# Filler products ahead of five attention stages, done as pairs on two halves of the PE array

## What is computed

```python
s = einsum('bqhgd,bkhd->bhgqk', qb, kb) * scale
p = softmax(where(mask, s, NEG))
o = einsum('bhgqk,bkhd->bqhgd', p, vb)
```

## Time and profile before

| | |
|---|---|
| median of 3 runs | 2260.39 us (2255.84 to 2262.58) |
| profiled execution, span | 2259.5 us |
| TensorE products busy | 2103.5 us, 93% |
| TensorE weight loads busy | 1715.7 us |
| VectorE busy | 894.1 us |
| ScalarE busy | 582.4 us |
| GpSimd busy | 1071.8 us |
| mean granted TensorE clock | 0.943 |

### The profile page before, as it was taken

How to read it: one execution, slowest core, us unless ns; L and a number is a source line. 1 busy time by engine, 2 the same in 40 slices (tenths; PEclk the granted TensorE clock), 3 DMA queues, 4 the chain that set the end, 5 groups by cost and what they waited for, 6 DMA issues and landing times.

```text
span 2259.5 us, 30914 instructions
## 1 busy us (share of the span) xinstructions
PE 2103.5 (93%) x10410; PEld 1715.7 (76%) x10420; DVE 894.1 (40%) x1703; ACT 582.4 (26%) x1432; POOL 1071.8 (47%) x688
## 2 busy tenths in 40 slices
PE   5776999789999989879999999999999999999999
PEld 4665676678888878766678888887787888888887
DVE  4663567264434015546654221201362644221200
ACT  2111556232222003336532011100132642011100
POOL 4443003257666655400135666665553036666664
PEclk9887998889999999988579999999999999999999
DMA  4222001113333322110012333332221013333322
GB/s 132 66 61 66 0 0 38 47 57 111 93 95 119 93 77 82 54 38 1 0 47 84 103 98 97 93 94 84 79 85 62 1 38 94 103 101 94 94 94 91
DMA packets 125209, 161.90 MB, mean 72 GB/s; under 512 B 11511, under 2 KB 87239, under 8 KB 125127
## 3 DMA queue, kind: packets, MB, share of 16 engines
q1 hardware_dynamic: 121440, 159.97, 23.0%
q10 hardware_dynamic: 3686, 0.82, 0.2%
HBM read 158.66 MB, written 2.10 MB: 71 GB/s over the span
## 4 chain that ended last, share of the span: by engine, by line
PE 87%; DVE 7%; ACT 2%; issue 2%; DMA 1%; POOL 1%; ACTq 0%; SPq 0%; DVEq 0%; POOLq 0%
PE ps L588 22%; PE ps L589 22%; PE ps L590 22%; PE ps L875 7%; PE ps L896 5%; PE ps L887 3%; PE ps L603 2%; PE ps L721 2%; PE ps L880 1%; DVE tok L1540 1%; PE ps L903 1%; DVE xt_lo L1550 1%; PE ps L1003 1%; DVE rstd L1516 1%; ACT dump L1114 1%
## 5 line engine op out<-in xcount | busy, mean ns | idle before, releaser
L420 POOL TENSOR_TENSOR w_lo<-raw,w_hi 128x1024 fp32r<-128x1024 f32 (+1 forms) x256 | 616.6, 2409 | 21.3
L418 POOL TENSOR_SCALAR w_hi<-raw 128x1024 fp32r<-128x1024 f32 (+1 forms) x256 | 275.0, 1074 | 557.6 <-PE ps L590 536.7
L588 PE MATMUL ps<-xt_hi,w_hi 128*128 128x512 f32 (+1 forms) x1160 | 433.6, 374 | 7.2 <-DVE xt_lo L1550 6.5
L589 PE MATMUL ps<-xt_lo,w_hi 128*128 128x512 f32 (+1 forms) x1160 | 432.7, 373 | 0.0
L590 PE MATMUL ps<-xt_hi,w_lo 128*128 128x512 f32 (+1 forms) x1160 | 432.6, 373 | 0.0
L588 PE MATMUL ps<-w_hi,xt_hi 128*128 128x512 f32 (+3 forms) x672 | 264.6, 394 | 28.3 <-ACT tok L1374 18.3
L589 PE MATMUL ps<-w_lo,xt_hi 128*128 128x512 f32 (+3 forms) x672 | 260.4, 387 | 0.0
L590 PE MATMUL ps<-w_hi,xt_lo 128*128 128x512 f32 (+3 forms) x672 | 260.1, 387 | 0.0
L588 PEld LDWEIGHTS ps<-xt_hi,w_hi 128*128 128x128 f32 x1160 | 219.8, 189 | 47.4 <-DVE xt_lo L1550 7.6
L590 PEld LDWEIGHTS ps<-xt_hi,w_lo 128*128 128x128 f32 x1160 | 219.6, 189 | 38.5
L589 PEld LDWEIGHTS ps<-xt_lo,w_hi 128*128 128x128 f32 x1160 | 219.7, 189 | 38.2
(11 more groups left out here) (268 smaller groups left out, 2799.1 us busy)
## 6 DMA issues: line engine op xcount, KB each, us to landing
raw<-in_w_up SPq DMA_DIRECT2D x88, 256.0 KB
raw<-in_l_w_gate SPq DMA_DIRECT2D x88, 256.0 KB
raw<-in_l_w_up SPq DMA_DIRECT2D x88, 256.0 KB
raw<-in_l_w_down SPq DMA_DIRECT2D x40, 512.0 KB
raw<-in_l_w_in SPq DMA_DIRECT2D x36, 512.0 KB
raw<-in_w_down SPq DMA_DIRECT2D x20, 512.0 KB
raw<-in_l_w_o SPq DMA_DIRECT2D x16, 512.0 KB
raw<-in_w_in SPq DMA_DIRECT2D x12, 512.0 KB
```

Of the source, the lines that this page charges most:

```text
L418: e.tensor_scalar(w_hi[:, s, 0:width], r, 1.0, 0.0, ALU.mult, ALU.add).then_inc(split, 1)
L420: e.tensor_tensor(w_lo[:, s, 0:width], r, w_hi[:, s, 0:width].bitcast(F32), ALU.subtract).then_inc(split, 1)
L588: e.matmul(o, s_hi, m_hi, start=start, stop=False)
L589: e.matmul(o, s_hi, m_lo, start=False, stop=False)
```

## The change

`fill(FILL, bank(6))` ahead of a stage becomes `warm(cfg["warm"])`, with a kind for each stage. All kinds write to PSUM places that nobody reads before they are overwritten. `low` and `high` are partitions (or columns) 0 to 63 and 64 to 127.

- nsa, "rows": four times two f32 products with 64 rows each, one from the low and one from the high partitions of `h`, 512 columns, into banks 6 and 7.
- swa, "columns": four times two f32 products with 64 stationary columns each, into the low and high partitions of bank 6, 512 columns.
- att2, "rounded": as "rows", from `ckv_hi`, which is fp32r.
- stk, "masked": twice two f32 products as in "rows", then a bf16 product of the identity with the mask onto each bank.
- fox, "steps": as "columns", but with 512, 384, 256 and 128 columns, two products each.

The fillers inside stk stay as they are. Nothing else changes.

```diff
--- before.py
+++ after.py
@@ -902,6 +902,32 @@
             for _ in range(times):
                 e.matmul(place, ident_b[:, :], dump[:, 0:W], start=True, stop=True)
 
+        def warm(kind):
+
+            low, high = slice(0, HD), slice(HD, P)
+            if kind == "rows":
+                for _ in range(FILL // 2):
+                    for b, half in ((6, low), (7, high)):
+                        e.matmul(bank(b), h[half, 0, 0:P], h[half, 0, 0:W], start=True, stop=True)
+            elif kind == "columns":
+                for _ in range(FILL // 2):
+                    for half in (low, high):
+                        e.matmul(ps[half, 6 * W:7 * W], h[:, 0, half], h[:, 1, 0:W], start=True, stop=True)
+            elif kind == "rounded":
+                for _ in range(FILL // 2):
+                    for b, half in ((6, low), (7, high)):
+                        e.matmul(bank(b), ckv_hi[half, 0:P], ckv_hi[half, :], start=True, stop=True)
+            elif kind == "masked":
+                for _ in range(FILL // 4):
+                    for b, half in ((6, low), (7, high)):
+                        e.matmul(bank(b), h[half, 0, 0:P], h[half, 0, 0:W], start=True, stop=False)
+                    for b in (6, 7):
+                        e.matmul(bank(b, P), ident_b[:, :], cfg["mask"][:, :], start=False, stop=True)
+            else:
+                for n in (4, 3, 2, 1):
+                    for half in (low, high):
+                        e.matmul(ps[half, 6 * W:6 * W + n * P], h[:, 0, half], h[:, 1, 0:n * P], start=True, stop=True)
+
         for s, v in cfg.get("start", ()):
             e.wait_ge(s, v)
         e.sem_inc(sem(f"{name}_pv"), 2)
@@ -909,7 +935,7 @@
             scores(0, k)
         for s, v in cfg["banks"]:
             e.wait_ge(s, v)
-        fill(FILL, bank(6))
+        warm(cfg["warm"])
         turn_probs(0, 0)
 
         def body(j, last):
@@ -924,19 +950,19 @@
         body(iters - 1, True)
 
     att = {
-        "nsa": dict(name="nsa", iters=8, look=3, dh=HD, band=False, mask=causal,
+        "nsa": dict(name="nsa", warm="rows", iters=8, look=3, dh=HD, band=False, mask=causal,
                     k=lambda hd: heads(kt1, hd // 4 + 2), v=lambda hd: columns(v1, hd // 4),
                     banks=[at("cat_fin", NT)]),
-        "swa": dict(name="swa", iters=4, look=3, dh=HD, band=True, mask=causal,
+        "swa": dict(name="swa", warm="columns", iters=4, look=3, dh=HD, band=True, mask=causal,
                     k=lambda hd: heads(kt1, hd // 4 + 6), v=lambda hd: columns(v1, hd // 4 + 4),
                     banks=[at("nsa_ofree", 66)]),
-        "att2": dict(name="att2", iters=4, look=3, dh=MQK, band=False, mask=causal,
+        "att2": dict(name="att2", warm="rounded", iters=4, look=3, dh=MQK, band=False, mask=causal,
                      k=lambda hd: heads(km, hd), v=lambda hd: columns(v2, hd),
                      start=[at("in2_tpa", 16), at("in2_tpd", 19), at("in2_copy", 32)], banks=[]),
-        "stk": dict(name="stk", iters=4, look=3, dh=HD, band=False, mask=strict,
+        "stk": dict(name="stk", warm="masked", iters=4, look=3, dh=HD, band=False, mask=strict,
                     k=lambda hd: heads(ksb, hd), v=lambda hd: columns(v2, hd + 8),
                     banks=[at("att2_ofree", 34)]),
-        "fox": dict(name="fox", iters=8, look=3, dh=HD + 2, band=False, mask=causal,
+        "fox": dict(name="fox", warm="steps", iters=8, look=3, dh=HD + 2, band=False, mask=causal,
                     k=lambda hd: heads(kf, hd), v=lambda hd: columns(v3, hd),
                     start=[at("in3_tpa", 16), at("in3_tpd", 16), at("in3_copy", 23)], banks=[at("in3_copy", 24)]),
     }
```

## The result

The changed kernel takes 2265.77 us (median of 14 runs, 2261.14 to 2272.97), the kernel before 2259.84 us in the same sessions (14 runs, 2255.84 to 2263.31). The ratio is 1.0026 with a 95% interval of 1.0017 to 1.0036, so +5.9 us (3.8 to 8.1). The forecast was 2265.7 us and +5.3.

The account below looks back on a forecast made before the run. TensorE's stream, busy 93% of the span, was taken as the bound. Overlapped terms nsa +2.4, swa +2.4, att2 -0.6, stk 0, fox +1.1 sum to +5.3 us on the median 2260.39: 2265.7 us, range 2256 to 2279.

Parts of the forecast that it names:

- The bound and the place: TensorE's stream bounds the kernel; old fillers lie on the path in nsa, swa, att2 and fox, behind a wait in stk.
- The price of an f32 product: All f32 fillers: 512 columns take 0.86 us, 0.43 us a pass, four times a bf16 filler's 0.22.
- The overlap: Fillers ahead of the stages: the two halves of a pair run side by side; +5.3 us in all, against +14.6 serial.
- low-1, low-2, high-1, high-2: Order of a pair's passes: high-1 runs beside low-2, high-2 beside the next low-1; four pairs take nine passes, not sixteen.
- The fixed 0.30 us: Change of shape around nsa's fillers: 0.20 us behind a 64-row product plus 0.10 us leaving the 128-row mask products.
- The term +2.4: Ahead of swa, as in nsa: overlapped column pairs add 2.4 us, serial ones 5.4 us, all on the path.
- a general 3 us either way: Whole kernel: allowance of 3 us for clock rises or falls moving against the shifted work.
- slower (0.48): Whole kernel: chance 0.48 of a time above 2267.2 us, beyond the 6.8 us bound.
- same (0.40): Whole kernel: chance 0.40 of overlap with a time within 0.3%, 6.8 us, of no change.
- rival A: Fillers ahead of the stages: pairs do not overlap, +14.6 us, 2275.0 us; chance 0.30.
- B: stk: masked fillers fill the stand-still and the clock stays at 2.4 GHz, gaining 18 us, 2248 us; chance 0.12.
- C: nsa, swa or fox: the clock falls behind half-array fillers, up to 56 us in nsa, around 2310 us; chance 0.05.

Follow-up runs that it names:

- e4: Kernel before, with the eight bf16 fillers ahead of each of the five stages done as four bf16 row pairs; 2280.3 us, ratio 1.0068.
- e9: Changed kernel, with swa's pairs by rows and both products of each on the low rows; 2296.0 us, ratio 1.0167.
- e5: Changed kernel, with the eight old bf16 fillers back in swa alone; 2264.0 us, ratio 1.0021.
- e12: Kernel before, with stk's eight fillers ahead replaced by twice one whole-array f32 product and one bf16 mask product; 2256.8 us, ratio 0.9987.
- e1: Changed kernel, with both products of every pair on the same half in all stages; ratio 1.0075 without the three longest runs.
- e7: Kernel before, with sixteen instead of eight bf16 fillers ahead of stk; 2260.6 us, ratio 1.0007.
- e2: Changed kernel without any fillers ahead of the five stages, those inside stk kept; 2276.5 us, ratio 1.0071.
- e6: Changed kernel, with both products of swa's pairs on the low columns; 2272.3 us, ratio 1.0059.

## Why the prediction was right, point by point

**The bound and the place.** Right. TensorE's stream sets the end, and lengthening it at four of five places lengthened the kernel; in stk the wait for ScalarE hid it.

**The price of an f32 product.** Right: 0.43 us a pass of 512 columns, four times a bf16 product. It alone explains why pairs that overlap fully still cost time. e4 is the counterpart, where pairing without f32 shortens nsa's gap from 1.80 to 1.13 us.

**The overlap.** Right in kind and a little too high in size. The step that failed is "the stream is low-1, low-2, high-1, high-2 ... Four pairs are then nine passes". The trace after has two passes starting 6 to 7 ns apart, and the next two 0.53 us later (0.43 further on). The rows don't name the half, but passes on one half start 0.43 us apart one by one (e9), so each two must be one pass of either half: low-1 with high-1, then low-2 with high-2. Whether the program or the engine puts them in that order isn't shown. A pair is two passes, four pairs are eight. With that one correction the forecast's own terms give 8 x 0.43 + 0.30 = 3.74 for nsa (3.80 measured), 2 x 0.43 + 0.4 = 1.26 for a round in stk (1.28, from 1058.29 to 1059.57), and 20 block passes x 0.107 + 0.3 = 2.44 for fox (2.45). The Trainium skill (TensorE: Matmul & The Clock Gate, Part 3) would have given a span of one product and some 4 ns for a pair, and the trace agrees with it: 6 to 7 ns. The forecast weighed that rule and took the dearer order; the rule was the better guide. The fixed 0.30 us was right to 0.06: 0.16 from the mask product to the first pass, 0.10 more between the first two starts than between later ones, and 0.10 on the way out.

**swa.** The term +2.4 measured +3.3 in the gap, +3.9 in the stage, and +1.1 more behind it. Its length should have been 3.8 as in nsa, +2.0; the rest is the clock, which I had priced only as a general 3 us either way.

**The sum.** Two errors cancelled: 0.4 us too much for each of nsa, swa and fox, and 1.3 us of clock too little in swa. Lengths alone are +4.2, with the clock +5.5, the forecast +5.3, the span +5.3, the median +5.9. The close hit is better than the method, and partly luck: outside the five gaps the profiled stretches moved by +1.1 and -0.9 us, and e5 and e12 show that medians and waits elsewhere move by 2 to 4 us. The chances, too, put slower (0.48) ahead of same (0.40), mostly for rival A, though the forecast's own +5.3 lay within the 6.8 us that it called no change, as +5.9 does.

**The rivals.** A (0.30) was wrong for this kernel; with the same half twice its prices were right: 7.22 us against 7.2 in swa (e9), 4.60 against 4.6 in fox and 2.19 against 2.1 in att2 (e1). B (0.12) was wrong: the clock fell in stk after the change too, and in e7. C (0.05) didn't happen here, but its mechanism is real and was priced too lightly: 20 us in e2 and e4, 29 in e9, over 90 in e1, against 56 at most in the forecast. That 56 rests on a misreading: it divides 96.7 us by stk's 8 heads, but this is only the part of stk at half clock. The whole stage is 110.6 us, 13.8 a head; less 1.7 for the inner fillers that is 12.1 against nsa's 6.9, or 83 us for sixteen heads. e1's nsa, less 13.2 us of fillers, took 194.8 us, 12.2 a head. With eight old fillers, or four f32 pairs on both halves, no run made was some 20 us longer, as it is when swa loses its clock. I had read the fillers as mere length on the path in nsa and swa, from a trace in which the clock happened to stay up. What the change risked was the clock, more than 5 us.

## What to carry to other kernels

A filler product has two prices: its length, read from the gap it stands in, and what the granted clock does with and without it, which only a run without it shows. Leave it out stage by stage, keep it where the clock falls and stays down (swa, 20 us for 1.75), and drop it where it lies on the path and holds nothing (nsa, att2, fox, inside stk: together 13 us). Two independent 64-row or 64-column products on opposite halves cost what one whole product costs (and 0.2 us a place for the change of shape), so pairing pays only if the element type and width stay the same; here f32 quadrupled what pairing halved.

## What the runs showed of the hardware that was not expected

- The halves of a pair interleave pass by pass: of two f32 products the first passes start 6 to 7 ns apart, and the second passes 0.43 us later (0.53 in the first pair).
- With serial half-row fillers 3 of 9 runs (e1) and 5 of 7 (e9) are longer by what a stage at half clock costs; the trace of one of the three shows it for nsa. With half-column work of the same count no run of 5 is (e6), and its trace shows the clock coming back during the fillers. The cause isn't shown.
- A TensorE busy without a break does not by itself get its clock back: 212.00 of 212.00 us busy at 0.50 in e1, 42.00 of 42.00 in e2.
- The 0.20 us that the earlier trace rows shows beyond a 64-row product's two passes has two parts: the second pass starts 0.53 us after the first, not 0.43, and the way back to 128 rows costs about 0.10 us. Eight passes in a row pay the first part once.
- A VectorE instruction of 128 x 2 takes 0.16 us, but up to 2.25 us while GpSimd is splitting weights. In the norms of the kernel before (the small instructions that make `sq_a` and `rstd`) 17 of 93 took over 0.5 us. Each of these started while an instruction of the split was running and ended within 0.04 us after it; none of the 75 under 0.2 us started inside one.
